# Second groups of the out and down projections as pairs of 64-row matmuls

## What is computed

```python
def swiglu(h, w_gate_up, w_down):
    gate, up = jnp.split(h @ w_gate_up, 2, axis=-1)
    return (jax.nn.silu(gate) * up) @ w_down

for layer in range(DEPTH):                       # DEPTH = 2
    hn = rms_norm(h, mix_norm[layer])
    if layer % 2 == 0:
        h = h + lru_dilated_mixer(hn, ...)       # ends with [rec, att] @ w_out, 1536 -> 1024
    else:
        h = h + swa_sink_mixer(hn, ...)          # ends with o @ w_out + b_out, 1024 -> 1024
    h = h + memory_cross_attention(...)          # ends with o @ wo, 512 -> 1024
    h = h + swiglu(rms_norm(h, ffn_norm[layer]), w_gate_up[layer], w_down[layer])
return rms_norm(h, final_norm)
```

## Time and profile before

| | |
|---|---|
| median of 3 runs | 1293.62 us (1293.11 to 1293.84) |
| span of the profiled execution | 1291.7 us |
| the median above that span | 1.9 us |
| TensorE matmul, busy | 1284.6 us (99%), 7548 matmuls |
| TensorE weight loads, busy | 1115.4 us (86%) |
| VectorE, busy | 914.6 us (71%) |
| ScalarE, busy | 537.0 us (42%) |
| GpSimd, busy | 251.7 us (19%) |
| mean granted TensorE clock | 0.999 of full speed |

### The profile page before, as it was taken

The page is one execution under the profiler, slowest core; times in us unless marked ns, Lnnn a source line. Parts: engine busy times, 40 slices in busy tenths (PEclk is TensorE's granted clock), DMA queues, the critical chain, the costliest instruction groups (busy, mean ns, idle before and its releaser), DMA issues.

```text
span 1291.7 us, 19977 instructions
## 1 busy us (share of the span) xinstructions
PE 1284.6 (99%) x7548; PEld 1115.4 (86%) x7548; DVE 914.6 (71%) x1461; ACT 537.0 (42%) x1130; POOL 251.7 (19%) x290
## 2 busy tenths in 40 slices
PE   9999999999999999999999999999999999999998
PEld 8888778888888998899988878888888998899986
DVE  7988856346689984388955778557789983489842
ACT  6347455124533560055612347425433650166512
POOL 0222154212322002100021226423221002000010
PEclk9999999999999999999999999999999999999999
DMA  7334322232433423333333341133333332333232
GB/s 249 98 98 114 90 71 94 82 98 82 131 91 96 123 83 98 98 115 104 103 90 114 108 117 57 50 98 98 99 98 98 115 99 93 98 121 99 83 98 98
DMA packets 96845, 130.73 MB, mean 101 GB/s; under 512 B 5328, under 2 KB 62160, under 8 KB 96752
## 3 DMA queue, kind: packets, MB, share of 16 engines
q1 hardware_dynamic: 94976, 127.29, 32.2%
q10 hardware_dynamic: 1776, 2.18, 0.6%
HBM read 124.67 MB, written 2.10 MB: 98 GB/s over the span
## 4 chain that ended last, share of the span: by engine, by line
PE 99%; DVE 0%; DMA 0%; ACT 0%; SPq 0%; issue 0%; DVEq 0%; ACTq 0%
PE ps L787 18%; PE ps L790 18%; PE ps L791 18%; PE ps L956 8%; PE ps L955 8%; PE ps L954 8%; PE ps L1440 1%; PE ps L1441 1%; PE ps L1437 1%; PE ps L1270 1%; PE ps L1286 1%; PE ps L1299 1%; PE ps L1159 1%; PE ps L1190 1%; PE ps L1177 1%; PE ps L1082 1%
## 5 line engine op out<-in xcount | busy, mean ns | idle before, releaser
L709 POOL TENSOR_SCALAR w_hi<-raw 128x1024 fp32r<-128x1024 f32 x156 | 178.7, 1146 | 939.0 <-PE ps L956 367.1
L1469 DVE TENSOR_TENSOR w_lo<-raw,w_hi 128x1024 fp32r<-128x1024 f32 x161 | 203.9, 1272 | 181.9 <-POOL w_hi L709 178.6
L787 PE MATMUL ps<-f_hi,w_hi 128*128 128x512 f32 x720 | 281.0, 390 | 0.2 <-DVEq L1865 0.2
L791 PE MATMUL ps<-f_hi,w_lo 128*128 128x512 f32 x720 | 280.2, 389 | 0.0
L790 PE MATMUL ps<-f_lo,w_hi 128*128 128x512 f32 x720 | 280.2, 389 | 0.0
L955 PE MATMUL ps<-zq_lo,quad_hi 128*128 128x256 f32 x896 | 253.6, 283 | 0.0
L954 PE MATMUL ps<-zq_hi,quad_hi 128*128 128x256 f32 x896 | 253.5, 283 | 0.0
L955 PEld LDWEIGHTS ps<-zq_lo,quad_hi 128*128 128x128 f32 x896 | 172.0, 192 | 0.2
L954 PEld LDWEIGHTS ps<-zq_hi,quad_hi 128*128 128x128 f32 x896 | 172.0, 192 | 0.2
L787 PEld LDWEIGHTS ps<-f_hi,w_hi 128*128 128x128 f32 x720 | 135.2, 188 | 28.8 <-DVEq L1865 0.4
L791 PEld LDWEIGHTS ps<-f_hi,w_lo 128*128 128x128 f32 x720 | 135.1, 188 | 28.4
(11 more groups left out here) (270 smaller groups left out, 2043.0 us busy)
## 6 DMA issues: line engine op xcount, KB each, us to landing
quad_raw<-in_w_gate_up SPq DMA_DIRECT2D x64, 512.0 KB
raw<-in_w_down SPq DMA_DIRECT2D x44, 512.0 KB
raw<-in_w_gate_up SPq DMA_DIRECT2D x48, 256.0 KB
raw<-in_w_out SPq DMA_DIRECT2D x20, 512.0 KB
raw<-in_w_in SPq DMA_DIRECT2D x19, 512.0 KB
raw<-in_xa_wkv SPq DMA_DIRECT2D x16, 512.0 KB
raw<-in_w_in SPq DMA_DIRECT2D x17, 256.0 KB
raw<-in_xa_wq SPq DMA_DIRECT2D x8, 512.0 KB
```

The lines of the kernel that those rows point to most:

```text
L709: pool.tensor_scalar(w_hi[:, slot], raw[:, slot], 1.0, 1.0, ALU.mult, ALU.mult).then_inc(s_hi, 1)
L787: ins = pe.matmul(o, whi, rhi, start=start, stop=False)
L791: return pe.matmul(o, wlo, rhi, start=False, stop=stop)
L1469: dve.tensor_tensor(w_lo[:, slot], raw[:, slot], w_hi[:, slot].bitcast(F32), ALU.subtract).then_inc(s_lo, 1)
```

## The change

`group` gets a switch `split`. With it, each product of 128 rows is made as two of 64 rows: partitions 0 to 63 (`e` = 0, the lower rows) and 64 to 127 (`e` = 1, the upper rows). They are not issued for the same output tile: the upper rows go to tile `x_`, the lower rows to tile `x_ + 2` modulo 4, so that the two matmuls that stand side by side write different banks. A unit has four such chunks `x_`, each of 2 contraction tiles x 3 matmuls x 2 halves, 12 matmuls. After two chunks each half comes to the tile that the other half wrote; therefore a chunk (except the first two of a group) waits with two new semaphores, one for each half, until the chunk before the last has ended. In the last unit tile 0 is told in the third chunk and tiles 1 to 3 at the end of the fourth.

`stage` passes `split=True` in the calls for remaining groups outside the loop. Those are the second groups of out0, xo0, down00, down01, out1, xo1 and down10. (The up stages have two remaining groups, which run in the loop `body`.) Nothing changes on the other engines.

```diff
+        s_half = [sem("s_lower_rows"), sem("s_upper_rows")]
...
+                    if split and not hook and not hooks and not before:
+                        for x_ in range(4):
+                            if j or x_ >= 2:
+                                pe.wait_ge(s_half[0], halves_told[0] - (j < units - 1 or x_ < 3))
+                                pe.wait_ge(s_half[1], halves_told[0] - (j < units - 1 or x_ < 3))
+                            told = j < units - 1 or x_ < 2
+                            halves_told[0] += told
+                            for kk in range(2):
+                                k = 2 * j + kk
+                                hi, lo = rhs(k)
+                                for y_ in range(3):
+                                    for e in range(2):
+                                        m = (x_ + 2 * (1 - e)) % 4
+                                        r = slice(HD * e, HD * e + HD)
+                                        w = (w_lo if y_ == 2 else w_hi)[r, half, kk, P * m:P * (m + 1)]
+                                        ins = pe.matmul(ps[:, bank(g_static, m), 0:n], w, (lo if y_ == 1 else hi)[r],
+                                                        start=k == 0 and y_ == 0 and x_ < 2,
+                                                        stop=k == 2 * units - 1 and y_ == 2 and x_ >= 2)
+                                        if x_ == kk == y_ == e == 0 and not (attention_told and j == 0):
+                                            ins.then_inc(s_used, 1)
+                                        if j == units - 1 and kk == 1 and y_ == 2 and (x_ == 3 or (x_ == 2 and e == 0)):
+                                            ins.then_inc(done, 1 + e)
+                                        elif told and kk == 1 and y_ == 2:
+                                            ins.then_inc(s_half[e], 1)
+                        continue
...
                         group(at_g + rest - 1, at_g + rest - 1, at_u + units * (rest - 1),
-                              at_u + units * (rest - 1), units, rhs, done)
+                              at_u + units * (rest - 1), units, rhs, done, split=True)
                 else:
                     for s in range(rest):
-                        group(at_g + s, at_g + s, at_u + units * s, at_u + units * s, units, rhs, done)
+                        group(at_g + s, at_g + s, at_u + units * s, at_u + units * s, units, rhs, done, split=True)
```

More of the change, by code:

```diff
@@ L791, in product @@
                 return pe.matmul(o, wlo, rhi, start=False, stop=stop)
+            halves_told = [0]
             def group(g_static, g, u0_static, u0, units, rhs, done, n=T, before=None, hook=None, first=0, last=None,
-                      attention_told=False, only=False, hook_at=None, hooks={}):
+                      attention_told=False, only=False, hook_at=None, hooks={}, split=False):
                 for j in range(first, units if last is None else last):
```

## The result

| | before | after |
|---|---|---|
| median of the runs | 1293.29 us (6 runs) | 1297.59 us (6 runs) |
| span of the profiled execution | 1291.7 us | 1295.6 us |
| TensorE matmul, busy | 1284.6 us, 7548 | 1288.3 us, 8292 |
| VectorE, busy | 914.6 us | 910.9 us |

The ratio of after to before is 1.0032, with a 95% interval from 1.0022 to 1.0043: 4.3 us slower, clear of no change. The forecast was +5.0 us (1298.6). The spans differ by 3.9 us, and that is what the two traces account for.

What follows compares the result with a forecast made beforehand. The prediction took TensorE's matmul stream (busy 1284.6 of 1291.7 us) to bound the kernel; 0.7 + 2.8 + 1.5 = +5.0 us on the median 1293.62 us gave 1298.6 us, range 1289.0 to 1308.5.

Steps and rivals of the forecast that it cites:

- term 1: Pace of pairs in the seven split groups: 744 pairs, each 1 ns slower than a full matmul's 227 ns, +0.7 us.
- term 2: TensorE changing between whole and half arrays, seven times in and out at 0.40 us each, +2.8 us.
- term 3: Tiles told later to VectorE, its first add moving 2.7 us; TensorE waits +1.5 us at xq1's sum of squares, behind out1.
- rival 1: In the split groups the extra 13.7 ns per matmul goes, 216 ns a pair: -3.8 us, 1289.8 us; chance 0.34.
- Term 4: Chunk waits, the instruction queue and semaphore telling inside the split groups cost nothing; 3 us per ns per instruction if uncovered.
- rival 2: In the split groups half of the extra goes, about 222 ns a pair: +0.2 us, 1293.8 us; chance 0.07.
- rival 3: In the split groups the halves pay the extra one after the other, 241 ns a pair: 1308.3 us; chance 0.08.
- rival 4: In the split groups fp32r halves don't run side by side, 2 x 227 ns a pair: +169 us, 1462; chance 0.05.
- the rule on weight loads and row groups: On TensorE, weight loads overlap running matmuls only where row groups differ; by it the pairs' pace would give near -8 us.

Runs made afterwards that it cites:

- e1: A kernel of TensorE streams alone, without the trunk's computation, one form of matmul per stream: 32 full fp32r matmuls 7.60 us, 32 pairs of 64 rows 7.61 us.
- e3: The changed kernel with only the last unit of the seven groups in pairs (168 pairs instead of 744), same late telling: 1297.28 us, ratio 1.0032.
- e4: The changed kernel with every second unit of the seven groups in pairs (16 stretches instead of 7, 384 pairs instead of 744): 1301.54 us, ratio 1.0062.
- e2: All matmuls on 128 rows as before the change, but the seven groups tell their tiles as late as the change does: 1294.66 us, ratio 1.0010.
- e7: TensorE streams alone, without the trunk's computation: strided and unstrided bf16, mixed types, and full matmuls alternating with pairs, the last 0.87 us a round.

## Why the prediction was right, and where it wasn't

The forecast of +5.0 us stands beside +4.3 measured. The mechanism of terms 1 and 2 is the one that the runs show; term 3 had its wait at the wrong place. That the sum came out so near is in part luck: term 1 was 0.7 us too large, term 2 0.5 too small, and term 3 0.8 too large.

**Term 1, the pace of a pair** (+0.7 us, from 228 ns; rival 1 had 216). Right, and for the reason given: plain fp32 shows no extra on full rows either, so pairs of it couldn't be the comparison. Pairs stand at 227 ns in the changed kernel, and in e1 each of three types has one number for both shapes. The term itself is 0 rather than 0.7: the 1 ns that I took from the difference of fp32 pairs and fp32 full rows lay within the resolution of those rows, and e1 has 429 ns for either.

**Term 2, the ways in and out** (+2.8 us at 0.40). Right in kind, too small: measured 0.49 in five groups and 0.43 in two, 3.3 us. e3 (same number of ways, a quarter of the pairs, same loss) and e4 (16 ways, +8.1 us) show that it is these that cost. The 0.40 was read at the attention scores and left out the matmuls that follow, of which a dozen stand up to 0.24 us apart instead of 0.227.

**Term 3, what is told later** (+1.5 us, all in xq1). The place was wrong, and the size is 0.7 us in the whole change, 1.6 where the late telling stands alone (e2). The step that failed is the reading of the earlier trace rows: I took the add at 861.64 for that of the fifth tile because it starts where the fifth tile is told. It was the fourth tile's, late by a low part of weights; the fifth tile's add is the one at 864.02, 2.4 us after the telling. The row of the kernel before, as it went on, has three adds more, so that the one at 864.02 is the fifth of eight; the last line is of xo0:

```profile
866.56 0.75 DVE L1515 SCALAR_TENSOR_TENSOR h<-ps,vec,h 128x512 f32<-128x512 f32 x1
...
870.09 0.74 DVE L1515 SCALAR_TENSOR_TENSOR h<-ps,vec,h 128x512 f32<-128x512 f32 x1
...
872.47 0.75 DVE L1515 SCALAR_TENSOR_TENSOR h<-ps,vec,h 128x512 f32<-128x512 f32 x1
...
359.55 0.68 DVE L1517 TENSOR_TENSOR h<-ps,h 128x512 f32<-128x512 f32 x1
```

So only 0.3 us of the 2.7 could reach the row behind out1, and 1 us of slack took it. The same slip in xo0: the add at 361.86 was the sixth; the fifth, at 359.55 before, had to wait until 361.67. There, where I had 0, the wait is 0.36 us, and in down01, where I had allowed 0 to 0.2, it is 0.30. The adds must be counted from the end of the row (eight tiles, a known pattern of low parts between them), not told by their times.

**Term 4** held: no wait inside the groups, and e3, with most of the waits for halves gone, is no faster by more than the measurement tells.

**Rivals.** 1 to 4 are ruled out by the pace: 227 ns is neither 216 nor 222, 241 or 454. The Trainium skill's fixed 2.5 ns beside a warm matmul's columns (TensorE: Matmul & The Clock Gate, Wait — 56ns, not 53.3ns?) agrees with bf16 here, 216 ns, as with plain fp32, and not with fp32r, 227 ns on full or half rows. By the rule on weight loads and row groups in the Trainium skill (TensorE: Matmul & The Clock Gate, Part 3, The mechanism), as the prediction worked it out, pairs would have won; they didn't, and no stream of e1 shows a gain by it.

## What to carry to other kernels

Splitting a full contraction into side-by-side halves adds nothing where the array is already full: the columns remain, the overhead of a matmul, here that of fp32r, goes with its type and is paid in each half at the same time, and each stretch costs its way in and out once. When a stream shows an overhead, compare it with a stream that differs in one thing alone (same rows, other type; same type, other rows) before building on the nearest row that lacks it. Before pricing a later signal, count which of the waiting engine's instructions waits for it.

## What was new about the hardware

- An fp32r matmul costs some 11 ns more than its columns and the 3 ns that bf16 shows beside them: 227 ns for 512 columns, on 128 rows, in pairs of 64 or in fours of 32, and 120 for 256 on 128 rows; bf16 216, plain fp32 429 a record of two passes (e1).
- A change between full and half rows costs 0.41 us there and back with one pair in it (e7), and 0.43 to 0.49 in the kernel, for 24 pairs as for 144.
- Behind a wait or a change of mode, the first dozen fp32r matmuls stand 224 to 240 ns apart before they settle at 227 (e1, and the changed kernel).
- A moving operand in bf16 with a stride of two takes 225 ns instead of 216, strided weights don't; changing between fp32r and bf16 costs some 20 ns there and back for one fp32r and two bf16, some 35 for eight and sixteen (e7).
